# Two transformer blocks on one core: grouped attentions multiply with the values held still, the row totals go round through DRAM

## The reference, cut to what matters

```python
sc = einsum('bqkgd,bskd->bkgqs', qi, ki) * scale - slopes * dist     # masked to -inf outside the window
p = softmax(concatenate([sc, sink_col]))[..., :-1]                   # total includes exp(sink - max)
y = einsum('bkgqs,bskd->bqkgd', p, vi)                               # then y @ w_proj (a) or [y, conv] @ w_out (c0, c1)
```

## Time and profile before

| | |
|---|---|
| time, median of 3 runs | 2526.25 us (2525.29 to 2527.48) |
| the profiled execution, its own time | 2525.54 us |
| its span, first to last instruction | 2523.7 us |
| busy: PE, DVE, ACT, POOL | 2496.8, 1189.6, 947.5, 182.6 us |
| attention a and its projections, 47 to 130 us | PE 75.75, DVE 41.67, ACT 57.82, POOL 7.32 us busy of 83 |
| attention c0 and the convolution, 1119 to 1212 us | PE 92.36, DVE 39.24, ACT 57.67, POOL 19.74 us busy of 93 |

### The profile page before, as it was taken

How to read it: one execution, slowest core, us unless ns; L and a number is a source line. 1 busy time by engine, 2 the same in 40 slices (tenths; PEclk the granted TensorE clock), 3 DMA queues, 4 the chain that set the end, 5 groups by cost and what they waited for, 6 DMA issues and landing times.

```text
span 2523.7 us, 28242 instructions
## 1 busy us (share of the span) xinstructions
PE 2496.8 (99%) x11504; PEld 2071.3 (82%) x11504; DVE 1189.6 (47%) x1595; ACT 947.5 (38%) x1398; POOL 182.6 (7%) x179
## 2 busy tenths in 40 slices
PE   9999999999999999999999999999999999999998
PEld 7878888888888888878888888888888788888887
DVE  6443454434475343454454444543444644544444
ACT  6668333322343232356432222422222464322222
POOL 2031010000020000011200000100000122000001
PEclk9999999999999999999999999999999999999999
DMA  7454433233223333245423332333332354332322
GB/s 197 109 124 118 134 108 100 92 100 101 92 84 109 93 99 94 89 130 130 115 95 100 93 99 89 99 97 99 94 101 87 112 142 117 100 99 93 100 90 78
DMA packets 78513, 265.33 MB, mean 105 GB/s; under 512 B 9648, under 2 KB 12976, under 8 KB 78000
## 3 DMA queue, kind: packets, MB, share of 16 engines
q1 hardware_dynamic: 69376, 233.57, 29.4%
q0 software_dynamic: 9008, 29.96, 6.0%
HBM read 234.56 MB, written 2.19 MB: 94 GB/s over the span
## 4 chain that ended last, share of the span: by engine, by line
PE 89%; DVE 4%; ACT 3%; issue 3%; POOL 0%; DMA 0%; SPq 0%; DVEq 0%; ACTq 0%; POOLq 0%
PE bank L769 28%; PE bank L770 28%; PE bank L771 28%; PE bank L810 2%; DVE w_lo L1091 2%; ACT w_hi L894 1%; PE bank L783 1%; PE bank L797 1%; DVE x L1207 1%; DVE z L1083 1%; ACT z L882 0%; POOL square_sum L1350 0%; DVE q L1158 0%; PE bank L843 0%; ACT h_hi L907 0%
## 5 line engine op out<-in xcount | busy, mean ns | idle before, releaser
L769 PE MATMUL bank<-h_hi,w_hi 128*128 128x512 f32 x2224 | 879.7, 396 | 2.7 <-DVE h_lo L1106 1.5
L771 PE MATMUL bank<-h_hi,w_lo 128*128 128x512 f32 x2224 | 867.2, 390 | 0.0
L770 PE MATMUL bank<-h_lo,w_hi 128*128 128x512 f32 x2224 | 867.0, 390 | 0.0
L1091 DVE TENSOR_TENSOR w_lo<-w_raw,w_hi 128x1024 fp32r<-128x1024 f32 (+2 forms) x392 | 485.3, 1239 | 318.3 <-ACT w_hi L894 317.9
L894 ACT ACTIVATE w_hi<-w_raw 128x1024 fp32r<-128x1024 f32 (+1 forms) x435 | 449.0, 1034 | 409.4 <-PE bank L771 407.3
L771 PEld LDWEIGHTS bank<-h_hi,w_lo 128*128 128x128 f32 x2224 | 417.9, 188 | 88.5
L769 PEld LDWEIGHTS bank<-h_hi,w_hi 128*128 128x128 f32 x2224 | 418.5, 188 | 86.9 <-DVE h_lo L1106 2.7
L770 PEld LDWEIGHTS bank<-h_lo,w_hi 128*128 128x128 f32 x2224 | 418.7, 188 | 80.8 <-issue 1.9
L769 PE MATMUL bank<-act_hi,w_hi 128*128 128x512 f32 x960 | 373.4, 389 | 0.0
L770 PE MATMUL bank<-act_lo,w_hi 128*128 128x512 f32 x960 | 373.4, 389 | 0.0
L771 PE MATMUL bank<-act_hi,w_lo 128*128 128x512 f32 x960 | 373.4, 389 | 0.0
(11 more groups left out here) (169 smaller groups left out, 1676.8 us busy)
## 6 DMA issues: line engine op xcount, KB each, us to landing
w_raw<-ffn_wg_dram SPq DMA_DIRECT2D x88, 512.0 KB, 3.5
w_raw<-ffn_wu_dram SPq DMA_DIRECT2D x88, 512.0 KB, 3.5
w_raw<-w_in_dram SPq DMA_DIRECT2D x67, 512.0 KB, 3.6
w_raw<-ffn_wd_dram SPq DMA_DIRECT2D x64, 512.0 KB, 3.5
w_lo<-w_raw POOLq DMA_DIRECT2D x51, 512.0 KB, 4.4
w_raw<-w_up_dram SPq DMA_DIRECT2D x32, 512.0 KB, 3.5
w_raw<-w_down_dram SPq DMA_DIRECT2D x32, 512.0 KB, 3.5
w_raw<-w_out_dram SPq DMA_DIRECT2D x24, 512.0 KB, 3.5
```

Of the source, the lines that this page charges most:

```text
L769: engine.matmul(to, w_hi[s][:, lhs], hi, start=k == 0, stop=False)
L770: engine.matmul(to, w_hi[s][:, lhs], lo, start=False, stop=False)
L771: product = engine.matmul(to, w_lo[s][:, lhs], hi, start=False, stop=job == "k_last")
L1091: engine.tensor_tensor(lo, value, hi.bitcast(F32), ALU.subtract).then_inc(signals[event].s, 1)
```

## The change

In a, c0 and c1 (not in b) the product with the values is turned round. The values, with high and low parts side by side (128 keys x 128 columns, made once for each attention by the new "v_lo"), are held, and the turned probabilities of all 4 heads of the group are streamed, 512 columns, first their high part and then their low part ("turn_lo" on DVE makes it, one slot behind "turn"). So rows 0 to 63 of the bank hold the product with the values' high part and rows 64 to 127 that with the low part. "pair" adds them: ACT copies the lower half out, DVE adds it to the upper half into half a tile `y`. Heads are now on partitions and queries along the free dimension, as the next projection wants them, so "turn_out" is gone. But the inverse totals are needed along the free dimension: "invert" (DVE, one slot behind the exps of g = 1) makes them, POOL stores them to DRAM turned (8 numbers from each of 128 partitions), and "inverse_in", 14 slots behind those exps, lets POOL fetch them spread over partitions, 64 at a time, in two DMAs. "weigh", 4 slots behind the last multiply, multiplies y by them on DVE; ACT copies the high part, and DVE makes the low part one slot later. Waits for statistics, banks and buffers are moved accordingly.

```diff
+        elif job == "exps" and key[0] in GROUPED and key[2] == 1:
+            self.later(1, "invert", *key[:2])
+            self.later(14, "inverse_in", *key[:2])
+        elif job == "turn" and key[0] in GROUPED:
+            self.later(1, "turn_lo", *key)
+        elif job == "v_turn" and key[1] is None:
+            self.later(1, "v_lo", *key)
+        elif job == "multiply" and key[0] in GROUPED and key[3] == len(CHUNKS[key[0]][key[1]]) - 1:
+            self.add("pair", key[:3])
+            if key[2] == 1:
+                self.later(4, "weigh", *key[:2])
+        elif job == "weigh":
+            self.later(1, "y_lo", *key)
...
-            self.later(at + delay + 2 * len(chunks) + 5, "turn_out", name, i)
+            if name == "b":
+                self.later(at + delay + 2 * len(chunks) + 5, "turn_out", name, i)
...
+                    if name in GROUPED:
+                        if c == 0:
+                            at = value_at["paired", key[:3]]
+                            pe.wait_ge(*done(*plan.values[at - 1]))
+                            pe.wait_ge(*done(*values_need(name)))
+                        at = chunk_at[key] % 2
+                        last = c == len(CHUNKS[name][i]) - 1
+                        pe.wait_ge(*done("turn_lo", key))
+                        engine.matmul(value_bank[:, :], values[name][:, chunk, g, :], turned_hi[name][:, at, :], start=c == 0, stop=False)
+                        engine.matmul(value_bank[:, :], values[name][:, chunk, g, :], turned_lo[name][:, at, :],
+                                      start=False, stop=last).then_inc(signals["multiplied"].s, 1)
+                        continue
...
+                elif job == "pair":
+                    name = key[0]
+                    act.wait_ge(*done("multiplied", (*key, len(CHUNKS[name][key[1]]) - 1)))
+                    if key in paired_before:
+                        act.wait_ge(*done("paired", paired_before[key]))
+                    engine.activation(lower_of[name], value_bank[HEAD:P, :], ACT.Copy).then_inc(signals["lower_copied"].s, 1)
+
+                elif job == "weigh":
+                    name, i = key
+                    act.wait_ge(*done("weighed", key))
+                    engine.activation(y_hi_of[name][:, :, block(i)], y_of[name].rearrange("p (t n) -> p t n", t=4), ACT.Copy).then_inc(signals["y_hi"].s, 1)
...
+                elif job == "pair":
+                    v.wait_ge(*done("lower_copied", key))
+                    engine.tensor_tensor(y_of[key[0]][half(key[2]), :], value_bank[0:HEAD, :], lower_of[key[0]], ALU.add).then_inc(signals["paired"].s, 1)
+
+                elif job == "invert":
+                    name, i = key
+                    total, inverse = row_sum[:, i % 2, :], row_inv[:, i % 2, :]
+                    v.wait_ge(*done("exped", (name, i, 1)))
...
+                    engine.reciprocal(inverse, total).then_inc(signals["row_inv"].s, 1)
+
+                elif job == "weigh":
+                    name, i = key
+                    spread, landed_at, count = inverse_in(name, i)
+                    v.wait_ge(*done("paired", (name, i, 1)))
+                    v.wait_ge(landed_at, count)
+                    engine.tensor_tensor(y_of[name], y_of[name], spread, ALU.mult).then_inc(signals["weighed"].s, 1)
...
+                elif job == "invert":
+                    name, i = key
+                    pool.wait_ge(*done("row_inv", key))
+                    engine.dma_start(dram["inverses"][inverse_at[key]].rearrange("h q -> q h"), row_inv[:, i % 2, :],
+                                     allow_slow_non_contiguous=True).then_inc(inverse_kept.s, 16)
+
+                elif job == "inverse_in":
+                    name, i = key
+                    n = inverse_at[key]
+                    spread, landed_at, _ = inverse_in(name, i)
+                    pool.wait_ge(inverse_kept.s, 16 * (n + 1))
+                    before = n - 1 if name == "a" else n - 2
+                    if before >= 0:
+                        pool.wait_ge(*done("weighed", plan.inverses[before]))
+                    for g in range(KV_HEADS):
+                        engine.dma_start(spread[half(g), :].rearrange("p (t n) -> p t n", t=GROUP),
+                                         dram["inverses"][n].rearrange("(t g) q -> g t q", g=KV_HEADS)[g].partition_broadcast(HEAD)).then_inc(landed_at, 16)
...
-    nc = bacc.Bacc("TRN2", target_bir_lowering=False, num_devices=1, dynamic_dma_scratch_size=4096)
+    nc = bacc.Bacc("TRN2", target_bir_lowering=False, num_devices=1, dynamic_dma_scratch_size=2048)
```

More of the change, by code:

```diff
@@ L126 @@
         "score": ("scored", "biased"), "mask_bias": ("bias_half", "bias_masked"), "softmax": ("sink_shift",),
-        "exps": ("exped",), "turn": ("turned", "turn_copied"), "multiply": ("multiplied",),
-        "normalise": ("row_total", "row_inv", "normalised"), "turn_out": ("turned", "y_hi"), "y_lo": ("y_lo",),
+        "exps": ("exped",), "turn": ("turned", "turn_copied"), "turn_lo": ("turn_lo",), "multiply": ("multiplied",),
+        "pair": ("lower_copied", "paired"), "invert": ("row_total", "row_inv"), "inverse_in": (), "weigh": ("weighed", "y_hi"), "v_lo": ("v_lo",),
+        "normalise": ("row_inv", "normalised"), "turn_out": ("turned", "y_hi"), "y_lo": ("y_lo",),
         "neg_sinks": ("neg_sinks",), "rel_bias": ("rel_spread",), "far_1": (), "far_2": (),
@@ L181, in run @@
             self.turns.append((job, key))
-        if job == "multiply" and key[2:] == (0, 0):
+        if job == "multiply" and key[0] in GROUPED and key[3] == 0:
+            self.values.append(("paired", key[:3]))
+        if job == "multiply" and key[0] == "b" and key[2:] == (0, 0):
             self.values.append(("normalised", key[:2]))
+        if job == "invert":
+            self.inverses.append(key)
         if job == "score":
@@ L196, in run @@
             self.later(2, "exps", name, i, g)
[L197 removed]
+        elif job == "exps" and key[0] in GROUPED and key[2] == 1:
[11 more added lines that the diff above has]
+            self.later(1, "y_lo", *key)
+        elif job == "multiply" and key[0] == "b" and key[2:] == (1, len(CHUNKS[key[0]][key[1]]) - 1):
             self.add("normalise", key[:2])
@@ L627, in two_blocks @@
         out_stored = signal("out_stored", 16)
+        inverse_kept = signal("inverse_kept", 16)
+        inverse_landed = [signal(f"inverse_landed{n}", 16) for n in range(2)]
         units = plan_units(dram)
@@ L681, in two_blocks, with inverse_in, statistics_free @@
         chunk_at = {key: n for of in plan.chunks.values() for n, key in enumerate(of)}
+        inverse_at = {key: n for n, key in enumerate(plan.inverses)}
+        paired_before = {}
+        for name in GROUPED:
+            of = [key for job, key in plan.values if job == "paired" and BUFFERS[key[0]] == BUFFERS[name]]
+            paired_before.update(zip(of[1:], of))
+        def inverse_in(name, i):
+            n = inverse_at[name, i]
+            spread = x[:, 7, :] if name == "a" else inverse_2[:, n % 2, :]
+            return spread, inverse_landed[n % 2].s, 32 * (n // 2 + 1)
+        def statistics_free(name, i):
+            if name in GROUPED:
+                return inverse_kept.s, 16 * (inverse_at[name, i] + 1)
+            return done("normalised", (name, i))
         def turn_freed(n):
@@ L687, in turn_freed @@
                 return done("mean_mixed", key)
-            return done({"v_turn": "v_copied", "turn": "turn_copied", "turn_out": "y_lo"}[job], key)
+            if job == "turn":
+                return done("turn_lo" if key[0] in GROUPED else "turn_copied", key)
+            if job == "v_turn":
+                return done("v_lo" if key[1] is None else "v_copied", key)
+            return done("y_lo", key)
         def score_free(n):
@@ L1295, in vector_program @@
                                          ALU.mult).then_inc(signals["normalised"].s, 1)
+                elif job == "y_lo" and key[0] in GROUPED:
+                    name, i = key
+                    v.wait_ge(*done("y_hi", key))
+                    rest(y_lo_of[name][:, :, block(i)], y_of[name].rearrange("p (t n) -> p t n", t=4), y_hi_of[name][:, :, block(i)], "y_lo")
                 elif job == "y_lo":
```

79 lines of the change are left out of this document (53 added, 26 removed).

## The result

The changed kernel took 2622.86 us (median of 4, 2622.31 to 2623.47) beside 2525.77 us for the kernel before on the same chip: ratio 1.0384, 95% interval [1.0371, 1.0396]. It is 97 us slower; 8 were forecast, and the time lies above the range.

What follows compares the result with a forecast made beforehand. The prediction took TensorE (PE), busy 99% of the span, as the bound. Saving 26.3 us against 34.7 us of new waits gave +8.4 us on 2525.54, so 2534 us, with an 8 in 10 range of 2506 to 2558 us.

Steps and rivals of the forecast that it cites:

- What it takes off PE: On PE in a, c0 and c1: cheaper "multiply" saves 21.1 us, dropping "turn_out" 5.2 us, in sum 26.3 us.
- The landing of the fetch: Inverse totals fetched on POOL's queue: there 4.0 us after the w_lo issue ends, range 2.45 to 7.2 us.
- its 34.7: New waits of PE in us: 11.7 in each of c0 and c1, 11.3 in a.
- The store: Inverse totals to DRAM on POOL: issue 3 us, landing 8 us, both ahead of "inverse_in"; cost nothing.
- So nothing: Cost of the store to the next w_lo addition behind it on POOL: none, with some 9 us of cover left.
- (C): Rival, slow small pieces: fetches at 7.2 us, 2560 us, or a store of 15.6 us, 2554 us; chance 0.17.
- the signs that the prediction named: In the traces: PE's neg_max waits 25 to 40 us; late w_lo or shifted SP fetches would show slow small pieces.
- The sentence on the Trainium skill, DMA: Bandwidth & Descriptors, Specifications: For the store: pieces under 512 B make the engine read, modify and write, pushing landing towards its upper bound, 15.6 us.
- The estimate of 7.4 us for the fetches: Two fetches on POOL's queue: 5.4 us from 512 packets at 10.5 ns, plus 2 us fixed.
- The 8.8 ns a piece: Pace of a row of sixteen issues on POOL, taken as close to the page's floor of 10.5 ns a packet.
- "pair" and turn_lo: On ACT and DVE: "pair" loses 3.7 us in a, block 2; turn_lo costs nothing, 7 us kept for the range.
- a sign of being wrong: In PE's waits: the prediction would be wrong if turn_lo showed as what PE waits for.

Runs made afterwards that it cites:

- e12: e1 without turn_lo and without ACT's copy of the lower half, "pair" also waiting for the block before to be read; 2508.63 us, ratio 0.9936.
- e3: The changed kernel with the store of inverse totals in dense order, 128 pieces of 32 B in place of 1024 of 4 B; 2588.31 us, ratio 1.0255.
- e9: e1 without ACT's copy of the lower half, DVE copying the upper half alone in "pair"; 2517.71 us, ratio 0.9969.
- e10: e1 without turn_lo, PE streaming the high part twice, "pair" also waiting for the block before to be read; 2525.1 us, ratio 0.9999.
- e1: The changed kernel without the store and fetches of the inverse totals, "weigh" multiplying by a tile already there; 2533.05 us, ratio 1.003.
- e8: The changed kernel with 20 dense-sized products put before the third score of group 1, blocks 1 to 3 of c0 and c1; 2622.61 us, ratio 1.0384.
- e7: a as before the change; c0 and c1 changed, with probabilities multiplied by inverse totals before the turn, no round trip; 2518.95 us, ratio 0.9973.

## Why the prediction was wrong

By its own steps:

**What it takes off PE: right.** 26.3 us were worked out; PE's busy time in e12 is 2471.2, 25.6 us under the earlier trace rows (0.7 us less than worked out). With hardly a wait, c0 and c1 gain 6.8 and 6.7 us of the 7.9 worked out for each (14 x 0.44 + 4 x 0.43). "multiply" is two products 0.23 us apart (1191.79 and 1192.02 in the changed kernel).

**The landing of the fetch: the step that failed.** 4.0 us after the w_lo issue were taken, 7.2 as the upper bound. From the end of the last w_lo issue to "weigh" it is 8.2, 6.1 and 8.5 us in blocks 0, 2 and 3 of c0. The bound came from landings in a queue without this store in it. The sign and the places were right (blocks 0, 2 and 3 wait), but block 1 was put at 0 and waits 6.61 us, and the four holds of PE in c0 sum to 30.0 us where 11.7 were forecast. In block 0 the 4.9 us forecast became 10.4: 4.2 are the later landing, and 1.3 that PE is at its third score 1.1 us after the start of the w_lo issue (1174.65 less 1173.55) where the prediction had 2.4 (1149.42 less 1147.02). c0's layer is 35.3 us slower; with the saving of 7.9 that is 43 us lost. Of it the round trip is 39.9 (+35.3 less -4.6), and 89 us over a, c0 and c1. The prediction had about 31 for it (its 34.7 less the 3.7 of "pair"). In a it was near, 7.6 us against 9.8; in c0 and c1 it had 23.4 against 79.5.

**The store: failed with it.** Its issue was taken as 3 us and is 0.94; its landing as 8 us, "ahead of inverse_in", and is 9.9 (within the bounds of 1.9 and 15.6). It isn't always over before the fetch: POOL waits for it ahead of 5 of the 12 pairs, 17.7 us in all. And it wasn't asked what the store does to the DMAs between: w_lo takes 8.1 us behind it instead of 4.4 to 5, and SP's load of weights behind w_lo moves onto the fetch. "So nothing" was 34.5 us by e3. The text had a rival for this, (C), with a chance of 0.17, and priced it at 20 to 26 us over the forecast; shown is its mechanism (e3), with more than its size. Of the signs that the prediction named, neg_max at 65.9 us instead of 25 to 40 and a late w_lo both point there.

The sentence on the Trainium skill, DMA: Bandwidth & Descriptors, Specifications, that small pieces make the engine read, modify and write, pointed to the right end of the range; the runs show 9.9 us for 1024 pieces of 4 B and 2.3 us for 128 of 32 B, not how the engine does it, and the piece size and the number of pieces change together in e3. The estimate of 7.4 us for the fetches, from the floor for each packet in the Trainium skill, DMA: Bandwidth & Descriptors, Bandwidth, is near the 8.2 us of block 0; but with the quick store of e3 the same fetches are there after 5.2, so these runs don't bear the floor out as the cause. The 8.8 ns a piece that the prediction set beside it were POOL's time to issue, not to move (the 1024 pieces of the store are issued in 0.94 us), and the closeness of the two was chance.

**"pair" and turn_lo: mis-sized.** "pair" in a was priced at 3.7 us, by a place on ACT ahead of the weight split; it stands behind kb_hi, vb and the split. turn_lo was put at nothing, with up to 7 us kept for the range. Measured by e9 and e10: 15.3 and 8.0 us, in all 24.4 (e12), of which 19.2 in a. In c0 and c1, where ACT has more room, both together cost 2.2 and 2.9 us. turn_lo shows by name in PE's waits, which the prediction had as a sign of being wrong: 7.8 us in e1 for turned_a_lo, 4.6 in e10 for ACT's copy in its place, with neg_max unchanged (21.3 and 21.7).

**The clock: not in the sum.** PE loses some 2.6 us behind a hold such as the first (an estimate: 5.1 us at half speed, from 1185.17 to 1190.3). Between e1 and the changed kernel PE's busy time grows by 24.5 us (2479.4 to 2503.9) with the same number of instructions, and its idle time by 64.9: the price of the round trip shows in two parts, and the prediction had only waits. They don't simply add, though: e8 gave 8.5 us of the busy time back, and the program got no shorter. How much of the 85 us would go with a clock that never falls is open.

**What is left.** Without round trip, ACT's copy and turn_lo (e12) a gains 3.4 us where 10.5 were worked out (20 x 0.44 + 4 x 0.43). "weigh", "invert" and the moved waits are candidates; no run parts them.

The sum, put together again: -26.3 for PE, +90 for the round trip (34.5 go with the store's small pieces, 5 stay when nobody waits; the two may overlap, and the rest is the wait for the fetches), +24.4 for pair and turn_lo, and the 9 us left open in a, c0 and c1: 97.

## What to carry to other kernels

A round trip through DRAM between two jobs of one pipeline is priced with everything that is in the same queue at that time, and the landing of each DMA is taken with the new ones ahead of it. Here the cut into pieces set that, not the bytes: the same 4 KB took 9.9 or 2.3 us. If a statistic is wanted along the other axis, first look for a place upstream where it still lies right: in c0 and c1 one DVE multiply per group took the place of three DMAs per block. And a link of 0.6 us through another engine's queue costs what stands ahead of it there (5.0 us in a), so a copy is cheap in one stage and dear in the next; decide stage by stage, as e7 does.

## What the runs showed of the hardware

- A store from 128 partitions in 1024 pieces of 4 B landed after 8.5 to 11.6 us; the same 4 KB in 128 pieces of 32 B after 1.7 to 4.1. Its issue on POOL took 0.935 us against 0.582, so the issue didn't tell of the landing.
- A DMA behind it on POOL's queue landed late: w_lo took up to 13.2 us (issued 2.2 us behind a store in c1), where the longest of the 51 is 6.3 us with the dense store.
- In the hold of c0 block 0 PE did nothing from 1174.8 on; the granted clock was 1.00 in the slice 1178 to 1180 and 0.52 in the next. PE worked again from 1185.2, and the clock was 0.50 up to 1190 and 0.92 in the slice 1190 to 1192. With 4.7 us of products put into the hold (e8) it was 0.96 from 1180 to 1185 and 0.70 from 1185 to 1190: the fall came later, not away.
